# Attention inside a one-layer encoder kernel: twelve more operands come from DRAM as 32x32 blocks and are turned by VectorE instead of TensorE

## The reference, cut to what matters

```
qa = rms_norm(gq...); ka = rms_norm(gk...)            # 8 query heads, 2 key heads, 64 wide, rotated
qm = concatenate([q_nope, q_pe], axis=-1)             # 8 latent heads, 64 + 32
km = concatenate([k_nope, broadcast(k_pe)], axis=-1)
sc = einsum('bqkgd,bskd->bkgqs', qblk, k) * scale     # per head: 4 blocks of 128 queries x 512 keys
p  = softmax(sc);  o = einsum('bkgqs,bskd->bqkgd', p, v)
```

## Time and profile before

| | |
|---|---|
| median of 3 runs | 1035.84 us (1035.31 to 1036.29) |
| profiled execution, its own time | 1036.18 us |
| its span in the profile | 1034.4 us |
| attention, first to last scores | 145.69 to 351.08 us |
| mean granted TensorE clock | 0.992 of full speed |

### The profile page before, as it was taken

The page is one execution under the profiler, slowest core; times in us unless marked ns, Lnnn a source line. Parts: engine busy times, 40 slices in busy tenths (PEclk is TensorE's granted clock), DMA queues, the critical chain, the costliest instruction groups (busy, mean ns, idle before and its releaser), DMA issues.

```text
span 1034.4 us, 15653 instructions
## 1 busy us (share of the span) xinstructions
PE 1005.1 (97%) x5055; PEld 806.5 (78%) x5055; DVE 851.3 (82%) x1064; ACT 760.3 (74%) x1022; POOL 483.4 (47%) x423
## 2 busy tenths in 40 slices
PE   8999999999999999995999999999999999999997
PEld 7999986666656688874888888888888888888885
DVE  6788778887888533378999999999999999999982
ACT  7665658888989745547787887778877888788772
POOL 2477679634687655427443244324442344324011
PEclk9999999999999999997999999999999999999999
DMA  9344240432343398854999999999999999999982
GB/s 329 68 123 130 82 161 11 129 66 64 123 128 72 125 252 239 233 147 147 394 393 403 398 408 410 402 400 397 420 401 401 398 419 400 402 397 410 412 337 41
DMA packets 109133, 276.02 MB, mean 267 GB/s; under 512 B 58321, under 2 KB 66732, under 8 KB 85404
## 3 DMA queue, kind: packets, MB, share of 16 engines
q1 hardware_dynamic: 103280, 258.11, 67.3%
q0 software_dynamic: 5744, 17.29, 6.7%
q10 hardware_dynamic: 60, 0.01, 0.0%
HBM read 247.46 MB, written 27.92 MB: 266 GB/s over the span
## 4 chain that ended last, share of the span: by engine, by line
PE 51%; DMA 1%; DVE 1%; issue 0%; ACT 0%; POOLq 0%; POOL 0%
PE ps L2213 11%; PE ps L2215 11%; PE ps L2214 11%; PE ps L2229 5%; PE ps L2227 5%; PE ps L2228 5%; PE ps L2180 1%; DMA out<-y,give 1%; DMA xt<-h,idxT 0%; DVE idx L1965 0%; DVE affT L1974 0%; DVE gates L1960 0%; POOLq L2487 0%; POOL out L2172 0%; ACT y L2341 0%
## 5 line engine op out<-in xcount | busy, mean ns | idle before, releaser
L2383 DVE TENSOR_TENSOR lo<-raw,hi 128x2048 fp32r<-128x2048 f32 x191 | 430.6, 2285 | 29.6 <-ACT hi L2305 29.4
L2305 ACT ACTIVATE hi<-raw 128x2048 fp32r<-128x2048 f32 x192 | 364.2, 1917 | 67.4 <-PE ps L2215 56.6
L2213 PE MATMUL ps<-hi,xehi 128*128 128x512 f32 x480 | 188.4, 393 | 0.1
L2215 PE MATMUL ps<-hi,xelo 128*128 128x512 f32 x480 | 187.1, 390 | 0.0
L2214 PE MATMUL ps<-lo,xehi 128*128 128x512 f32 x480 | 186.7, 389 | 0.0
L2137 POOL DMA_INDIRECT xe<-h,take x60 | 110.7, 1845 | 25.1 <-issue 13.7
L2132 POOL COPY take<-idx 128x4 uint32 (+1 forms) x15 | 31.0, 2067 | 188.6 <-DVE xt L2399 188.3
L1471 DVE TENSOR_REDUCE nmax<-ps 128x1 f32<-128x512 f32 x128 | 85.9, 681 | 28.3 <-PE ps L1300 15.1
L2215 PEld LDWEIGHTS ps<-hi,xelo 128*128 128x128 f32 x480 | 90.1, 188 | 19.1
L2213 PEld LDWEIGHTS ps<-hi,xehi 128*128 128x128 f32 x480 | 90.3, 188 | 18.6 <-issue 0.5
L2214 PEld LDWEIGHTS ps<-lo,xehi 128*128 128x128 f32 x480 | 90.2, 188 | 18.3
(11 more groups left out here) (311 smaller groups left out, 2061.2 us busy)
## 6 DMA issues: line engine op xcount, KB each, us to landing
raw<-in_w_down SPq DMA_DIRECT2D x64, 1024.0 KB, 10.3
raw<-in_w_gate SPq DMA_DIRECT2D x60, 1024.0 KB, 10.5
raw<-in_w_up SPq DMA_DIRECT2D x60, 1024.0 KB, 10.0
w_raw<-in_w_in SPq DMA_DIRECT2D x8, 592.0 KB, 8.4
x<-in_x SPq DMA_DIRECT2D x8, 512.0 KB, 5.3
r<-reciprocal_sums SPq DMA_DIRECT2D x32, 128.0 KB, 3.0
attention_out<-pj SPq DMA_DIRECT2D x16, 256.0 KB, 2.3
woraw<-in_w_o SPq DMA_DIRECT2D x4, 1024.0 KB, 6.1
```

Of the source, the lines that this page charges most:

```text
L2213: pe.matmul(ps[:, dst[n], :], rowhi[:, c, :], hi[w][:, cols], start=c == 0, stop=False)
L2215: last = pe.matmul(ps[:, dst[n], :], rowlo[:, c, :], hi[w][:, cols], start=False, stop=c == KD - 1)
L2305: act.activation(hi[s][:], raw[r][:], ACT.Copy).then_inc(hi_done, 1)
L2383: dve.tensor_tensor(lo[s][:], raw[r][:], hi[s][:].bitcast(F32), ALU.subtract).then_inc(lo_done, 1)
```

## The change: what it does

Six grouped query pairs (heads 4-5 and 6-7 of the first set and all four pairs of the second) and all six pairs of paired keys are no longer transposed by TensorE. They join the latent queries: 28 items are loaded from DRAM as blocks and turned by VectorE, sixteen of them as before (three loads) and twelve new ones (four loads each, 128 rows). The first two query pairs, all grouped keys and the unpaired latent keys stay with TensorE. The first set's operands are already in DRAM (`first_pj`, `first_kv`). For the second set SP stores two more arrays at n = 1, so that it issues twelve stores there in place of four. The table `loads_in` says in which round n of SP's loop an item is loaded, before or after the round trip of the reciprocals. `turn_at` puts each turn one unit before its item is due. `qT` stays one tile: a turn waits until the last user of the item in front of it is done.

```diff
@@ -130,6 +130,8 @@
     pj_dram = nc.dram_tensor("first_pj", [P, TS, C_CQ], F32).ap()
     q_dram = nc.dram_tensor("latent_q", [SETS, P, TS, MH * QK], F32).ap()
     kv_dram = nc.dram_tensor("first_kv", [P, TS, KV_ROW], F32).ap()
+    pq_dram = nc.dram_tensor("second_pq", [P, TS, C_K], F32).ap()
+    kn_dram = nc.dram_tensor("second_kn", [P, TS, K_NOPE], F32).ap()
 
     with ExitStack() as ctx:
         sb = lambda name, shape, dt=F32: ctx.enter_context(nc.sbuf_tensor(name, shape, dt))
...
@@ -1040,9 +1042,13 @@
             preps.append(("k", g + 1))
         preps.append(("q", g))
     prep_index = {p: n for n, p in enumerate(preps)}
-    latent_query = lambda kind, g: kind == "q" and g % HEADS >= QH
-    transposed = [sum(1 for p in preps[:n + 1] if not second(*p) and not latent_query(*p)) for n in range(len(preps))]
-    latent_heads = [g for g in range(ALL) if latent_query("q", g)]
+    by_blocks = lambda kind, g: kind == "q" and g >= GROUP or paired(kind, g)
+    transposed = [sum(1 for p in preps[:n + 1] if not second(*p) and not by_blocks(*p)) for n in range(len(preps))]
+    block_items = [p for p in preps if by_blocks(*p) and not second(*p)]
+    item_of = {p: block_items.index((p[0], p[1] - second(*p))) for p in preps if by_blocks(*p)}
+    users = [[prep_index[p] for p in preps if item_of.get(p) == m] for m in range(len(block_items))]
+    squares = lambda kind, g: QK // SQUARE if kind == "q" and g % HEADS >= QH else P // SQUARE
+    blocks_in = [sum(squares(*p) for p in block_items[m % 2:m + 1:2]) for m in range(len(block_items))]
 
     buffer_of, last_head, freed = {}, {}, {}
     for g in range(ALL):
@@ -1072,6 +1078,11 @@
     q_turned = sem("q_turned")
     qb, qT = att["qb"], att["qT"]
 
+    loads_in = {1: ((2,), ()), 2: ((3,), ()), 3: ((4, 5), (6,)), 4: ((7, 8), (9,)), 5: ((10, 11), (12,)), 6: ((13, 14), ()),
+                7: ((15,), ()), 8: ((16,), ()), 9: ((17,), ()), 10: ((18,), ()), 11: ((19, 20), (21,)), 12: ((22, 23), (24,)),
+                13: ((25, 26), (27,))}
+    assert [m for n in sorted(loads_in) for part in loads_in[n] for m in part] == list(range(2, len(block_items)))
+
     def rows_of(g):
         return att["rows"][g // HEADS]
 
@@ -1115,20 +1126,31 @@
                 sp.dma_start(att["r"][n % 2][e * VD:(e + 1) * VD, :],
                              r_dram[n, e].rearrange("p i -> (p i)").partition_broadcast(VD)).then_inc(r_loaded[n % 2], 16)
 
-        def store_queries():
+        def store_rows():
+            pj, q_rows, kv_rows = att["rows"][1]
+            sp.wait_ge(rows_ready, T)
             for i in range(TS):
-                sp.dma_start(q_dram[1, :, i, :], att["rows"][1][1][:, i].rearrange("p h c -> p (h c)")).then_inc(q_stored, 16)
-
-        def load_queries(g):
-            m = latent_heads.index(g)
+                sp.dma_start(pq_dram[:, i, :], pj[:, i, 0:C_K]).then_inc(q_stored, 16)
+                sp.dma_start(q_dram[1, :, i, :], q_rows[:, i].rearrange("p h c -> p (h c)")).then_inc(q_stored, 16)
+                sp.dma_start(kn_dram[:, i, :], kv_rows[:, i, 0:K_NOPE]).then_inc(q_stored, 16)
+
+        def load_blocks(m):
+            kind, g = block_items[m]
+            h, first = g % HEADS, g < HEADS
             if m >= 2:
                 sp.wait_ge(q_turned, m - 1)
-            if m == MH:
-                sp.wait_ge(q_stored, W_LOADED + 16 * TS)
-            for a in range(QK // SQUARE):
-                c = (g % HEADS - QH) * QK + a * SQUARE
-                sp.dma_start(qb[m % 2][a * SQUARE:(a + 1) * SQUARE],
-                             q_dram[g // HEADS, :, :, c:c + SQUARE].rearrange("(b s) i r -> s i b r", s=SQUARE)).then_inc(qb_loaded[m % 2], 16)
+            if not first and block_items[m - 1][1] < HEADS:
+                sp.wait_ge(q_stored, W_LOADED + 16 * 3 * TS)
+            if kind == "k":
+                rows, at = kv_dram if first else kn_dram, place(h) * NOPE
+            elif h < QH:
+                rows, at = pj_dram if first else pq_dram, h * HD
+            else:
+                rows, at = q_dram[g // HEADS], (h - QH) * QK
+            for b in range(squares(kind, g)):
+                c = at + b * SQUARE
+                sp.dma_start(qb[m % 2][b * SQUARE:(b + 1) * SQUARE],
+                             rows[:, :, c:c + SQUARE].rearrange("(b s) i r -> s i b r", s=SQUARE)).then_inc(qb_loaded[m % 2], 16)
 
         def store_heads(n):
             s, c = n // KD, n % KD
@@ -1144,20 +1166,20 @@
             sp.dma_start(wo["raw"][:, 2 * (i % 2):2 * (i % 2) + 2, :],
                          a["w_o"].rearrange("(k p) n -> p k n", p=P)[:, 2 * i:2 * i + 2, :]).then_inc(wo_loaded, 16)
 
-        load_queries(QH)
-        load_queries(QH + 1)
+        load_blocks(0)
+        load_blocks(1)
         for n in range(HEAD_PAIRS):
-            first = HEADS + QH if n == HEADS // 2 - 2 else 2 * n + 4
-            if first % HEADS > QH or n == HEADS // 2 - 2:
-                load_queries(first)
-                load_queries(first + 1)
+            for m in loads_in.get(n, ((), ()))[0]:
+                load_blocks(m)
             if n == HEADS // 2:
                 sp.wait_ge(o_added, HEADS)
                 load_output_weights(0)
                 load_output_weights(1)
             spread_reciprocals(n)
+            for m in loads_in.get(n, ((), ()))[1]:
+                load_blocks(m)
             if n == 1:
-                store_queries()
+                store_rows()
             if n == HEADS // 2 + 1:
                 load_output_weights(2)
             if n:
@@ -1259,7 +1281,7 @@
 
     def tensor_program(pe, first_key, finish_tile, product, route_rest):
         def prepare(kind, g):
-            if second(kind, g) or latent_query(kind, g):
+            if second(kind, g) or by_blocks(kind, g):
                 return
             n = prep_index[kind, g]
             pj, _, kv_rows = rows_of(g)
@@ -1353,8 +1375,8 @@
         def prepare(kind, g):
             n = prep_index[kind, g]
             h = g % HEADS
-            if latent_query(kind, g):
-                act.wait_ge(q_turned, latent_heads.index(g) + 1)
+            if by_blocks(kind, g):
+                act.wait_ge(q_turned, item_of[kind, g] + 1)
             else:
                 act.wait_ge(prep_ready, transposed[n])
             if kind == "q":
@@ -1365,7 +1387,7 @@
                 dst = khi[buffer_of[g]]
                 if g in freed:
                     act.wait_ge(score_ready, freed[g])
-            src = qT if latent_query(kind, g) else ps[:, PREP, :]
+            src = qT if by_blocks(kind, g) else ps[:, PREP, :]
             if h < QH and kind == "q":
                 part = slice(HD, P) if second(kind, g) else slice(0, HD)
                 act.activation(dst[part, :], src[part, :], ACT.Copy, scale=float(HD) ** -0.5).then_inc(prep_hi, 1)
@@ -1454,14 +1476,14 @@
                 dve.scalar_tensor_tensor(out=lo[0:QK, :], in0=src[0:QK, :], scalar=k["gcol"][0:QK, gain:gain + 1],
                                          in1=hi[0:QK, :].bitcast(F32), op0=ALU.mult, op1=ALU.subtract).then_inc(prep_lo, 1)
 
-        def turn_queries(g):
-            m = latent_heads.index(g)
-            dve.wait_ge(qb_loaded[m % 2], W_LOADED + 16 * (QK // SQUARE) * (m // 2 + 1))
+        def turn_blocks(m):
+            rows = squares(*block_items[m]) * SQUARE
+            dve.wait_ge(qb_loaded[m % 2], W_LOADED + 16 * blocks_in[m])
             if m:
-                dve.wait_ge(prep_lo, prep_index["q", latent_heads[m - 1]] + 1)
-            dve.transpose(qT[0:QK, :], qb[m % 2][0:QK].rearrange("p i b r -> p (i b r)")).then_inc(q_turned, 1)
-
-        turn_at = {u - 1: g for u, listed in due.items() for kind, g in listed if latent_query(kind, g)}
+                dve.wait_ge(prep_lo, users[m - 1][-1] + 1)
+            dve.transpose(qT[0:rows, :], qb[m % 2][0:rows].rearrange("p i b r -> p (i b r)")).then_inc(q_turned, 1)
+
+        turn_at = {u - 1: item_of[p] for u, listed in due.items() for p in listed if p in block_items}
         LAST = T - 1
         prepare("k", 0)
         prepare("q", 0)
```

More of the change, by code:

```diff
@@ L330, in build @@
         project_and_attend(nc, a, x_dram, k, temps, w, att, wo, pj, q_rows, kv_rows, w_raw, uq_raw, ukv_raw,
-                           ps, banks, o_dram, r_dram, wo_loaded, pj_dram, q_dram, kv_dram,
+                           ps, banks, o_dram, r_dram, wo_loaded, pj_dram, q_dram, kv_dram, pq_dram, kn_dram,
                            moe, out_rows, h2_rows, raw_loaded, out, h2_dram)
@@ L1010, in project, with attend @@
     return (sync_program, gpsimd_program, tensor_program, scalar_program, vector_program), signals
-def attend(phase, project_signals, a, k, att, wo, ps, banks, o_dram, r_dram, q_dram, wo_loaded):
+def attend(phase, project_signals, a, k, att, wo, ps, banks, o_dram, r_dram, pj_dram, q_dram, kv_dram, pq_dram, kn_dram, wo_loaded):
     rows_ready, mla_ready, kv_done, proj_done, row_copied, pj_back, mla_back, xlo_done, clo_done, ones_ready = (
```

(7 more changed lines are left out.)

## The result

The changed kernel takes 1057.79 us (median of 6 runs, 1053.51 to 1061.38) beside 1036.08 for the kernel before on the same chip: ratio 1.0211, 95% interval 1.0200 to 1.0223. It is slower, as forecast, but by 21.7 us and not by 8, and it lies outside the range of 1036 to 1050. The profiled execution has a span of 1056.0 us, 21.6 more than before, with a mean granted TensorE clock of 0.982.

The account below looks back on a forecast made before the run. It took TensorE (97% busy) as the bound, with the chain max, exponential, next scores nearly as full. Terms -1.0 - 0.15 + 2.0 + 0.9 + 0.4 + 4 x 0.7 + 3.0 = +7.95 us gave 1043.8 us, range 1036 to 1050.

Parts of the forecast that it names:

- a paired key in no special place: Keys 12, 14, 28 and 30: late load 0.3 us plus chain, 0.7 us lost for each of the four.
- The places where loads would be late: Query 9 (+2.0 us), keys 10-11 (+0.9, and 0.4 for the chain) and keys 26-27 (+3.0, chain included).
- so it lands about 3 us behind them ... at 196.5: Query 9's load, queued behind the twelve stores ending at 193.4, lands at 196.5; wanted at 194.54, VectorE waits 2.0 us.
- my upper bound of 5: Query 9's wait at most 5 us, if the stores run at three quarters of the rate and end 3 us later.
- One cost at nothing: Low halves now reading `qT` and the high half, both in SBUF, 24 new ones: taken as no cost.
- rival 3: Second set: DVE and POOL's shared access decides; two keys each cost up to 2.3 us more, 1048.4 us; chance 0.12.
- the chain's 0.7: Paired key: its turn on VectorE delays ACT's exponential and the next scores, 0.4 us net; 0.7 including 0.3 late load.
- the wait for the load covers it: Key 26: slower low halves out of SBUF cost nothing extra, being hidden in the wait for its late blocks.
- The grouped queries' -1.15: Grouped query pairs gain TensorE time: 1.0 us in the second set, 0.15 us in the first.
- Rival 1: TensorE's saved 5.3 us come through, 1030.5 us, or 1033 with half the relief; chance 0.16 together.
- Rival 2: All loads are in time and only the chain counts: +1.3 us, 1037.1, or 1039 with one late load; chance 0.24.
- rival 4: The forecast's own sum, with late loads and chain costs: 1040 to 1047 us; chance 0.48.

Follow-up runs that it names:

- the first experiment: The changed kernel with query 9's block loads issued before the twelve stores instead of behind them: 1059.44 us, ratio 1.0216 to the kernel before.
- turned_into_psum: The changed kernel with only the destination of the twelve new turns changed, to the PSUM bank TensorE had used: 1050.32 us, ratio 1.0139.
- keys_into_psum: keys_alone_mended with the keys turned into PSUM and the latent query behind them turned ahead of the keys' low halves: 1034.15 us, ratio 0.9975.
- nine_items_psum: Kernel before with six paired keys and query pairs 6, 16, 18 by blocks, turned into PSUM, mended, pair 16's blocks asked for earlier: 1038.24 us, ratio 1.0019.
- first_queries_on_pe: The changed kernel with loads in time, splits moved, keys turned earlier, and query pairs 4 and 6 left to TensorE: 1040.76 us, ratio 1.0040.
- all_three: The changed kernel with mended loads, moved output-weight splits and keys turned two units ahead, together: 1042.27 us, ratio 1.0060.
- keys_alone_mended: The changed kernel with only the six paired keys by blocks, loads in time, splits moved, keys turned two units ahead: 1038.57 us, ratio 1.0022.

## Why the prediction was wrong

**What held.** The direction; the 0.70 us of a turn with 128 rows (0.707 on average); the price of a paired key in no special place (0.7 forecast, 0.7, 1.1 and 0.5 measured for keys 12, 14 and 28), and its form: unit 44 starts 1.13 us behind unit 43, unit 47 2.19 us behind 46, with PE idle 0.81 us for the exponential. The places where loads would be late were the right ones, all three (a fourth wait, 1.45 us for pair 16's blocks, moved no unit). And a us at the attention's end was a us at the end of the kernel, within 0.8.

**Query 9: the step that failed is "so it lands about 3 us behind them ... at 196.5".** The stores themselves took what the sum gave them: SP had issued the twelfth by 193.07, where the sum had 193.4. But the store of a head pair stood behind them until 194.1, the three loads were then issued one after the other until 196.5, and the last landed 4.51 us behind its issue at 195.84 and not about 3: at 200.35. A wait of 5.54 in place of 2.0, beyond even my upper bound of 5. That the queue and not the item is the cause, the first experiment shows.

**"One cost at nothing" is the step that failed most.** I excused the low halves out of SBUF place by place, keys 28 and 30 not at all, and put the term at nothing. turned_into_psum changes only where the new turns write, and gives 7.5 us back, the lower clock behind them included. The mechanism was in the forecast as rival 3, with a chance too low. Its price for the low halves was right where it struck: keys 30's took 3.84 us in place of 1.52, 2.3 more. With the chain's 0.7 and 2.6 at the lower clock behind it, a term that no rival had, that makes the 5.6 measured. The Trainium skill ("SBUF — State Buffer", section "SBUF: two separate sides") speaks of a lock held for a whole instruction when a DVE operation has two SBUF inputs and a GpSimd operation reads SBUF. By that rule, the trace agrees: low halves of 64 rows from SBUF take 939 ns on average in the changed kernel, and the one at keys 30 that met POOL's subtraction 2.74 us, ending 0.54 us behind it; from PSUM they take 746 in turned_into_psum.

At keys 26 the excuse ("the wait for the load covers it") was right for the changed kernel, but it also means that the late load hid the collision: with the blocks in time 3.9 of the 4.9 us stayed, and the moved splits took another 2.9 away.

**The clock was in no term.** With each of the three long waits of TensorE its clock fell to 1.2 GHz for 6.83 us. In such a stretch a unit takes 2.15 us where it took 1.13 or 1.24. At keys 30 that was 2.6 us of the 5.6 (units 120 and 121), at keys 26 2.4 of 4.9, at units 36 to 39 some 2 to 2.7 of 7.5: together about 7 of 21. These shares are read from unit starts, and they belong to the same losses that the paragraphs above name; no run changed the clock alone.

**The grouped queries' -1.15.** TensorE's relief came, 0.40 to 0.44 us at units 20, 61, 68 and 77 (and 1.01 at unit 13), but it went again. Units 15 and 16 took back 1.06 us, with the turned tile in PSUM too; their cause is open. At unit 28 ACT waits 2.37 us for POOL, which the low halves out of SBUF had held up (one of its operations beside such a half took 1.08 us in place of 0.73); with the tile in PSUM it waits 1.37, and unit 28 loses 0.25 in place of 1.28. At units 79 to 96 of the second set a part went in the output weights' loads behind the block loads. That I had looked at only as a lack of ACT's time.

**The rivals.** Rival 1 was false of this kernel: neither of its conditions, the key handed over in time and the loads in time, was met. keys_into_psum brings both about, and there TensorE's relief does come through, key by key. Rival 2 fell at once. What decided was rival 3 at keys 30 and the late loads of rival 4 at query 9, keys 10 and keys 26, which I had priced as alternatives, and behind both the clock.

## What to carry to other kernels

Ask of a moved operation where its result lies, not only which engine does it: a tile in PSUM, out of GpSimd's way, gave back 7.5 of 21.7 us with nothing else changed, and with the loads in time and the order around it mended, a kernel with half of the items was 0.25% faster than the one before, though what of that the items themselves gave is not shown. Price a transfer by its place in the queue that issues it, with every store ahead of it and a landing under load, and look at which transfers are now behind it. When the busiest engine has to wait some us, add what it does at the lower clock afterwards. Costs of different mechanisms at one place are no alternatives: they may add up (keys 30: chain, collision and clock) or one may hide the other until it is mended (keys 26).

## What the runs showed of the hardware

- Within the attention, over all runs, each wait of TensorE of 2.42 to 6.74 us came with a stretch of 3.41 or 6.83 us at 1.2 GHz, which began between 2.7 us before and 1.7 us after the end of the wait. Of the waits of 1.7 to 1.9 us some were followed by such a stretch (1.73 in nine_items_psum, 1.89 in first_queries_on_pe) and some not (1.88 in all_three, 1.91 in keys_alone_mended).
- VectorE's 32x32 transpose of 128x512 fp32 took 0.69 to 0.71 us into SBUF and 0.71 to 0.73 us into PSUM.
- A low half of 64x512 took 0.70 to 0.76 us from PSUM even beside GpSimd, and up to 2.75 us from SBUF beside GpSimd's subtraction (two: 3.84 us). GpSimd was held up too: its subtraction took 2.69 us there and 2.38 with the tile in PSUM.
- In the changed kernel a block load of 64 KB mostly landed 2.4 to 3.0 us behind its issue, query 9's 2.8 to 4.5 us behind the twelve stores, and keys 26's 4.7 to 5.3 us behind a load of 1 MB.
